# Second projection: six value tiles plain and first, then 21 pairs by seven half products, with queries and keys among them

## What is computed

```
def _odd_layer(x, segs, S0, pre_g, post_g, w_in, w_out, a_up, a_b, g_norm_g):
    hn = _rmsnorm(x, pre_g).astype(x.dtype)
    proj = jnp.einsum('bld,de->ble', hn, w_in).astype(F32)
    q, k, v, r, alow = _split(proj, ODD_SPLITS)      # 1024, 1024, 2048, 2048, 16 features
    qh = _heads(q, G_HEADS) * (G_DK ** -0.5)
    lg = jax.nn.log_sigmoid(jnp.einsum('blr,rk->blk', alow, a_up.astype(F32)) + a_b.astype(F32)) / G_TAU
...
    # _gla_segment, per chunk:
        b = jnp.cumsum(gc, axis=2)
        qd = qc * jnp.exp(b)
        A = jnp.einsum('bhtd,bhjd->bhtj', qd, kc * jnp.exp(-b))
```

## Time and profile before

| what | value |
|---|---|
| time, median of 3 runs | 2100.09 us (2096.57 to 2101.86) |
| time of the profiled execution | 2102.05 us |
| span of its core | 2100.3 us |
| mean granted TensorE clock | 0.983 of 2.4 GHz |
| PE busy | 2028.6 us, 97% of the span |
| DVE / ACT / POOL busy | 1246.1 / 792.6 / 266.8 us |

### The profile page before, as it was taken

The page is one execution under the profiler, slowest core; times in us unless marked ns, Lnnn a source line. Parts: engine busy times, 40 slices in busy tenths (PEclk is TensorE's granted clock), DMA queues, the critical chain, the costliest instruction groups (busy, mean ns, idle before and its releaser), DMA issues. The chain is left out here.

```text
span 2100.3 us, 33193 instructions
## 1 busy us (share of the span) xinstructions
PE 2028.6 (97%) x12862; PEld 1804.5 (86%) x12862; DVE 1246.1 (59%) x2213; ACT 792.6 (38%) x1476; POOL 266.8 (13%) x378
## 2 busy tenths in 40 slices
PE   7999999999999899999969999999999799999997
PEld 7999999999999677787659999999999677777774
DVE  5466676645564666666656557676655465455543
ACT  6555543323231544444335344332212343333323
POOL 0000000000000621111100000000000452323222
PEclk9999999999999899999979999999999899999999
DMA  3121232443333754554342332444334554545442
GB/s 141 56 65 50 66 101 76 150 154 94 113 104 99 236 167 145 169 169 151 93 136 76 94 92 78 135 146 135 110 97 116 180 173 164 183 165 181 162 153 72
DMA packets 210407, 264.92 MB, mean 126 GB/s; under 512 B 49284, under 2 KB 157060, under 8 KB 208216
## 3 DMA queue, kind: packets, MB, share of 16 engines
q1 hardware_dynamic: 210264, 262.95, 39.9%
HBM read 172.91 MB, written 89.99 MB: 125 GB/s over the span
## 5 line engine op out<-in xcount | busy, mean ns | idle before, releaser
L588 DVE TENSOR_TENSOR pa_stage<-pa_ps,pa_stage 128x536 f32<-128x536 f32 x110 | 77.0, 712 | 119.3 <-PE pa_ps L555 111.0
L588 DVE TENSOR_TENSOR pc_stage<-pc_ps,pc_stage 128x536 f32<-128x536 f32 x110 | 77.0, 712 | 97.3 <-PE pc_ps L555 77.6
L402 PE MATMUL pa_ps<-a_XT_hi,pa_w_hi 128*128 128x358 f32 x576 | 133.2, 340 | 0.3 <-PEq L209 0.3
L402 PE MATMUL pa_ps<-a_XT_hi,pa_w_lo 128*128 128x358 f32 x576 | 125.9, 327 | 0.0
L402 PE MATMUL pa_ps<-a_XT_lo,pa_w_hi 128*128 128x358 f32 x576 | 125.8, 326 | 0.0
L1477 PE MATMUL mc_ps<-mc_wout_hi,mc_mix_hi 128*128 128x512 f32 x256 | 105.9, 414 | 5.0 <-POOL mc_mix_lo L3193 5.0
L555 PE MATMUL pc_ps<-c_XT_hi,pc_w_hi 128*128 128x268 f32 x384 | 110.2, 287 | 0.0
L555 PE MATMUL pa_ps<-a_XT_hi,pa_w_lo 128*128 128x268 f32 x384 | 110.1, 287 | 0.0
L555 PE MATMUL pc_ps<-c_XT_hi,pc_w_lo 128*128 128x268 f32 x384 | 110.1, 287 | 0.0
L555 PE MATMUL pc_ps<-c_XT_lo,pc_w_hi 128*128 128x268 f32 x384 | 110.1, 287 | 0.0
L555 PE MATMUL pa_ps<-a_XT_lo,pa_w_hi 128*128 128x268 f32 x384 | 110.0, 287 | 0.0
(11 more groups left out here) (576 smaller groups left out, 5948.2 us busy)
## 6 DMA issues: line engine op xcount, KB each, us to landing
pa_w_raw<-in_w_a SPq DMA_DIRECT2D x57, 512.0 KB, 4.6
pc_w_raw<-in_w_c SPq DMA_DIRECT2D x49, 512.0 KB, 4.6
scr_c<-pc_stage SPq DMA_DIRECT2D x48, 512.0 KB, 3.2
scr_a<-pa_stage SPq DMA_DIRECT2D x40, 512.0 KB, 3.2
mc_sample_state<-in_s SPq DMA_DIRECT2D x32, 512.0 KB, 4.6
out_s_s<-mc_sample_state SPq DMA_DIRECT2D x32, 512.0 KB, 2.8
ma_sample_state<-in_c SPq DMA_DIRECT2D x32, 257.0 KB, 4.1
out_c_s<-ma_sample_state SPq DMA_DIRECT2D x32, 257.0 KB, 3.0
```

The source lines that it names most:

```text
L402: ins = pe.matmul(self.ps[:, 3 * s + t, 0:TC], w[:, k, :], x[:, k, t * TC:(t + 1) * TC], start=(k == 0 and j == 0), stop=(k == KT - 1 and ...
L588: dve.tensor_tensor(dst, self.out(p, product), x, ALU.add).then_inc(self.added, 1)
```

## The change

Only six value tiles stay plain, and they come first (`C_PLAIN = 6`). Then follow 21 pairs: 8 of a query tile above a key tile, 8 gated ones, 5 of values. A pair of query and key takes its decays in the pair itself, by a multiplication in the staging tile (`decay`) behind its last add. `soft` and `chain` for channel tile p+1 stand in pair p, for p from 1 to 6, and `exps` for p at the head of pair p; the first two chains are made among the plain tiles. For this banks 6 and 7 are kept for the gate rounds during pairs 0 to 7 (`narrow`), which leaves three PSUM slots to the products: each waits for the product three before. A gate round is two matmuls of 512 columns, and its last 48 columns are made once, for six tiles together. All token sums now fall in the time of six plain tiles. `sum_weights` moves from DVE to POOL, in both projections. The output weights are loaded in pairs 9 to 13.

```diff
-    def sum_weights(self, dve, p):
+    def sum_weights(self, pool, p):
...
+        q = self.at(p, product) - 1
+        if q < self.narrow:
+            s = (2 - q) % 3
+        elif self.narrow:
+            s = (3, 0, 2, 1)[(q - self.narrow) % 4]
...
-    def products(self, pe, p):
+    def products(self, pe, p, hook=None):
         for i, name in enumerate(self.order(p)):
             q = 7 * p + i
-            if q == 2:
+            if i == 1 and hook:
+                hook()
+            if q == (1 if self.narrow else 2):
                 pe.wait_ge(self.G.psum_free[0], (self.first + 1) // 2)
-            if q >= 4:
-                self.wait_read(pe, (q - 4) // 7, int(self.order((q - 4) // 7)[(q - 4) % 7]))
+            before = q - 3 if q < self.narrow else q - 4
+            if before >= 0 and q != self.narrow:
+                self.wait_read(pe, before // 7, int(self.order(before // 7)[before % 7]))
...
             self.add(dve, p, 5, lower[1], lower[0], 1)
+            middle()
             self.add(dve, p, 3, upper[1], lower[1], 3)
-            if more:
-                self.sum_weights(dve, p + 1)
...
+        if early:
+            between()
         if more:
             self.split_sums_lo(dve, p + 1)
-        between()
+        if not early:
+            between()
...
-C_TILE = [C_V0 + 16 + 2 * p for p in range(8)] + [C_V0 + 2 * p for p in range(8)]
+C_PLAIN = 6
+C_TILE = [1 + 2 * p for p in range(8)] + [C_V0 + 16 + 2 * p for p in range(8)] + [C_V0 + C_PLAIN + 2 * p for p in range(5)]
...
+                HP.t_his(act, 0)
+                HP.t_his(act, 1)
+                soft(0)
+                v_tile(1)
+                exps(0)
...
                 for p in range(NPAIR):
...
+                    if 1 <= p < 8:
+                        exps(p)
                     HP.copies(act, p, upper, lower)
                     if p + 1 < NPAIR:
                         HP.split_upper_hi(act, p + 1)
+                    if 1 <= p < 7:
+                        soft(p + 1)
...
+                def decay(p, m):
+
+                    dve.wait_ge(exps_ready, p + 1)
+                    dve.wait_ge(HP.added, HP.ready(p)[m])
+                    x = flat[m][:, 0:T]
+                    if m == 0:
+                        ins = dve.scalar_tensor_tensor(out=x, in0=x, scalar=DK ** -0.5, in1=eqf, op0=ALU.mult, op1=ALU.mult)
+                    else:
+                        ins = dve.tensor_tensor(x, x, ekf, ALU.mult)
+                    ins.then_inc(qk_ready, 1)
...
+                    HP.sums_of(dve, p, upper, lower, p + 1 < NPAIR, lambda: finish(p, 0),
+                               (lambda: chain(p + 1)) if 1 <= p < 7 else (lambda: None), p < 8)
```

More of the change, by code:

```diff
@@ L663, in copies, with sums_of @@
         self.copy(act, p, 1, upper[0])
-    def sums_of(self, dve, p, upper, lower, more, between):
+    def sums_of(self, dve, p, upper, lower, more, between, middle=lambda: None, early=False):
         def into(x, y, after):
@@ L2409, in _ @@
                 G.load(sp, 2, 0)
-                def pair(i):
-                    n, h, d = 2 * i + 1, i // 2, i % 2
-                    if i < 7:
+                for i in range(C_PLAIN // 2):
+                    n = 2 * i + 1
+                    if n + 2 < C_PLAIN:
                         G.load(sp, n + 2, 1)
@@ L2481, in pair, with v_tile @@
-                    if i < 7:
-                        G.split_hi(act, n + 3, 0, i + 2)
-                for i in range(8):
-                    pair(i)
+                    act.activation(ekf, bsum, ACT.Exp, scale=-1.0 / 16).then_inc(exps_ready, 1)
+                def v_tile(n):
+                    s = n % 2
+                    act.wait_ge(G.gemm_done, n + 1)
+                    if n >= 3:
+                        act.wait_ge(spilled[s], 32 * ((n - 1) // 2))
+                    act.activation(stage[s][:], G.bank(s), ACT.Copy).then_inc(v_ready, 1)
+                    act.wait_ge(v_ready, n)
+                    act.sem_inc(G.psum_free[s], 1)
+                    if n + 2 <= C_PLAIN:
+                        G.split_hi(act, n + 2, s, (n + 2) // 2)
@@ L2538, in pair @@
                                                   op0=ALU.min, op1=ALU.subtract))
[L2539 removed]
+                    if i:
                         dve.wait_ge(exps_ready, i)
@@ L2574, in pair, with token_sums @@
-                    dve.wait_ge(qk_ready, 2 * i + 2)
-                    dve.sem_inc(G.psum_free[0], 1)
-                    if i < 7:
-                        G.split_lo(dve, n + 3, 0)
-                for i in range(8):
-                    pair(i)
+                def token_sums(i):
+                    HP.t_sums(dve, i)
+                    HP.t_lows(dve, i)
+                token_sums(0)
+                token_sums(1)
+                chain(0)
+                G.split_lo(dve, 3, 1)
+                token_sums(2)
@@ L2591, in gate, with finish @@
                     dve.sem_inc(sig_read, 1)
-                for p in range(NPAIR):
-                    if p and head_of(p - 1)[0]:
-                        gate(p - 1, 1, flat[1])
-                    HP.sums_of(dve, p, upper, lower, p + 1 < NPAIR, (lambda: gate(p, 0, flat[0])) if head_of(p)[0] else (lambda: None))
+                def finish(p, m):
+                    if kind_of(p)[0] == "qk":
+                        decay(p, m)
+                    elif kind_of(p)[0] == "gated":
+                        gate(p, m)
```

237 lines of the change are left out of this document (133 added, 104 removed).

## The result

The changed kernel takes 2123.21 us (median of 4 executions, 2119.11 to 2123.95); the kernel before took 2100.98 us beside it. The ratio is 1.0095, 95% interval 1.0083 to 1.0106: slower, by 22 us in the medians and by 20 us in the ratio. The profiled execution took 2123.95 us, with a span of 2122.2 us where that of before was 2100.3.

What follows compares the result with a forecast made beforehand. PE's matmul count times pace was taken to bound the kernel. Terms -14.5 + 0.2 + 6.7 + 1.9 + 1.3 + 2.3 + 23.0 gave +20.9 us on 2102.05 profiled: 2123, or 2121 by the median, range 2106 to 2132.

Steps and rivals of the forecast that it cites:

- Plain tiles: Second projection: ten plain tiles become five pairs, each 20.8 us against 23.7 for two plain tiles, 14.5 us less.
- Head: Start of second projection: PE's third gate round waits 6.7 us for ACT's read, plus 2.3 us of lowered clock.
- the term of 1.9 us: Value tile 3's third gate round waits behind ACT's token sums, copy and weight split: 1.9 us late (bounds 0 and 3).
- Three slots: Pair 0 of the second projection: the fourth product waits for ACT's copy of the first, +1.3 us (0 to 2).
- The loop: Query and key pairs: SP, ACT, DVE latencies of 24.2 us plus 1.0 blocking, 25.2 a pair; six waits, +23.0 us.
- The clock in the pairs: Query and key pairs: 2.3 us of slower matmuls fit inside each 3.9 us PE wait and cost nothing more.
- What costs nothing: POOL's sums in gated, value and first-projection pairs: covered by two products, 5.9 us, before product 6; later output-weight load also free.
- my own sign of being wrong: New profile: PE waits in the first projection or pairs beyond 8, listed as a sign of C.
- A: Rival: query and key pairs don't stall, each taking PE's 21.3 us; only the head remains, 2098 us; chance 0.08.
- B: Rival: loop as in A and ACT's first gate-round read at the head not late, -13, 2087 us; chance 0.05.
- C: Rival: POOL and DVE block 2.6 us a pair, or first projection too, 2131; both projections' gated pairs stalling 2140; chance 0.13.
- D: Rival: no mutual block of POOL and DVE, load a microsecond sooner; loop 23.2 us, total 2109 us; chance 0.14.

Runs made afterwards that it cites:

- the last experiment: The changed kernel with two more 128x512 tensor_tensor on POOL ahead of each pair's weight sums, pairs 2 to 8 of the second projection: 2144.52 us, ratio 1.0192.

## Why the prediction was right

The forecast was 2121 us, the result 2123, by the mechanism it named. Step by step, against the traces:

*Plain tiles.* Five value pairs take 104.0 us, as against 118.4 for ten plain tiles (10 x 72 x 0.1645): -14.4, predicted -14.5.

*Head.* The wait is 6.51 us (6.7 predicted), and the window 1130.80:1137.40 has a clock of 0.56, so of 6.6 us about 2.9 are lost (2.3 predicted). Tile 3's third round does not wait at all: the term of 1.9 us was mis-sized and is 0. That the first stall, which I had not put ahead of it in that layout, gave ACT the time to catch up is a guess that no run tests.

*Three slots.* PE waits 1.7 us for ACT's copy in pair 0, and 0.6 before; the pair is 1.2 us longer (1.3 predicted). In the kernel before, the same edit costs 6 us, by waits of 3.45 and 0.74 us and a lower clock: the term is right here and would not be elsewhere.

*The loop.* Pair by pair 26.1, 25.7, 25.2, 26.0 and 25.4, 25.7 on average; predicted 25.2. In pair 3 its steps measure: decay to split 5.97 (5.6), split 0.96 (1.0), soft with Exp and Ln 4.85 (4.5), chain 6.87 (5.7, and 1.0 for blocking set apart), three adds 2.07 (2.1), upper decay to add of product 4 3.66 (3.9, in the cycle before), lower decay 1.28 (1.4): 25.66. The chain's 1.17 us more are its first instruction (1.47) and its scan (3.37 us, 2.39 where POOL is idle), and the run with DVE's sums in the same order, where the chain takes 5.69 us, confirms it. So blocking costs 1.2 us a pair on the path, where I took 1.0. In total pairs 2 to 7 and the wait ahead of pair 2 cost 149.5 - 6 x 20.8 - 5 x 0.46 + 3.0 = 25.4 us, 23.0 predicted; the run without the decay work takes 24.6 us off the pairs.

The Trainium skill, "SBUF — State Buffer", section "Who interferes with whom", has the second of two such instructions block for the whole of the first: the scan's 0.98 us more, less than one POOL instruction of 1.3, agrees, and so do POOL's own 2.17 and 2.33 beside a DVE subtraction and the chain.

*The clock in the pairs.* The prediction said that a lower clock fits inside the waits. It does, and it changes how they look. After the wait of 3.07 us the clock is at 0.50, the level of 1.2 GHz, and the next wait is only 1.52 us, after which it stays at 1.00:

```profile
1270.70:1276.50 5.80, 5.80 (x25) 5.79 (x26) 5.70 (x6) 0.00 (x0) 0.00 (x0) 0.50 0.36 95
1296.30:1299.30 3.00, 3.00 (x24) 3.00 (x25) 2.96 (x4) 0.00 (x0) 0.00 (x0) 1.00 0.00 0
```

The period is 25.7 us with the slow stretch and 25.2 without, and 25.2 to 26.1 over all five: the loop sets it, not PE's pace. The sum of PE's waits, 15.3 us, is thus less than what the loop costs. The rest is nearly all slow clock: behind the waits ahead of pairs 2, 3, 5 and 6 stretches of 4.6, 5.8, 6.1 and 4.0 us have clocks of 0.63, 0.50, 0.50 and 0.57, in which 9.4 us are lost. Whoever reads the waits alone finds 15 of 25 us.

*What costs nothing.* The one step that failed in kind: POOL's sums in the first projection, and the wait of PE there was my own sign of being wrong. The 16 pairs there take 1.0 us longer (335.1 against 334.1), and up to 3.8 us longer in the other nine traces with the same sums there. The wait stands where I had put the cover, before product 6 of pair 1, which is due at 381.5:

```profile
379.80 1.49 ACT L507 ACTIVATE pa_w_sums_hi<-pa_w_sums 128x1536 fp32r<-128x1536 f32 x1 [6.30 <-POOL pa_w_sums L489]
...
383.22 0.36 PE L562 MATMUL pa_ps<-pa_t_hi,pa_w_sums_hi 128*128 128x268 f32 x1 [1.67 <-DVE pa_w_sums_lo L511]
```

The two products cover 5.9 us. But the loads of pair 1 land so late that POOL starts at 373.75, 1.7 us ahead of the pair, and its sums (6.0 us, the first 2.16 beside DVE's low part), ACT's 1.49 and DVE's 1.76 end at 383.07, 7.7 us into the pair. I had taken them to be done when the pair begins or just after. In the later pairs PE has no such wait. Before, with four sums on DVE, the same wait is 0.3 us.

*The sum.* The terms as measured, -14.4, 6.5, 2.9, 0, 1.2, 25.4 and 1.0, with my 0.2 for the gate rounds, give 22.8 us; the spans differ by 21.9. So that the total came within 2 us is in part luck: the head cost 1.5 us less than forecast (9.4 against 10.9), the loop 2.4 more, and the first projection 1.0 that I had put at nothing.

The rivals: A and B would have needed the loop at 21.3 us, which only the run without decay work has; the one with another order and no sums on POOL comes close, at 21.4 to 21.8. Of C (more blocking, or a stall of the first projection too) only the stall came, 1.0 us; its 2.6 us of blocking a pair did not. D was wrong in both parts: the load took 5.97 us, and the blocking costs 1.2.

Left open: why the store of a lower tile lands a microsecond later in some pairs; how the 13.6 us of the last experiment divide into blocking and later loads, since both belong to it; and what a fourth slot would do in the changed kernel. With four, product 1 would wait for the add of product 5, which stands ahead of the chain. No run tries this; the banks are taken by the gate rounds.

## What to carry to other kernels

When several engines pass one piece of work round once per iteration, add up the loop's latencies before trusting any engine's busy share: here no engine but PE was over 75% busy in a pair, and PE still lost 4.4 us in each. Such a loop can be cut by order, without removing work: the load put ahead of the stores in one queue gave 10 to 12 us, all the reorderings 16, the head 6.5, and the saving of the change itself (14.4 us) only then showed. Moving work to an idle engine is not free if the two block each other or if a consumer waits for the slower result: the four sums take 2.6 us on DVE and 6.0 on POOL, and cost 7 us on POOL in the kernel before, 7 us on DVE inside the loop, and little on DVE in the good order. And two kernels whose medians differ by a few microseconds are better compared stage by stage in their traces.

## What the hardware showed that I had not expected

After a wait of 3.02 us the clock was 0.63 over the next 4.6 us, after 3.71 us it was 0.50 over the next 6.1; after 1.76 us it was 0.57 over 4.0 us, yet after a longer wait of 2.25 us it stayed at 1.00. So the length of one wait does not by itself tell what the clock will do. The rows, of the changed kernel:

```profile
1244.60:1249.20 4.60, 4.60 (x25) 4.60 (x26) 4.60 (x5) 0.00 (x0) 0.00 (x0) 0.63 0.25 71
...
1321.50:1327.60 6.10, 6.07 (x26) 5.97 (x27) 5.92 (x6) 0.00 (x0) 0.00 (x0) 0.50 0.33 90
1347.60:1351.60 4.00, 4.00 (x20) 4.00 (x21) 3.98 (x4) 0.00 (x0) 0.00 (x0) 0.57 0.14 38
1372.90:1376.00 3.10, 3.08 (x24) 3.08 (x25) 3.03 (x4) 0.00 (x0) 0.00 (x0) 1.00 0.00 0
```
